# Latent attention of a two-block transformer: query squares summed on GpSimd, value blocks paired in one bank and copy, next query weights split behind the copies

## The chip, the cores and the metric

The kernel runs on one core of a Trainium2 chip. The metric is the device time of one execution in microseconds (us), the median of the runs. The five engines of a core work from queues of their own and wait for one another through semaphores: TensorE (PE; its weight loads are shown as PEld), VectorE (DVE), ScalarE (ACT), GpSimd (POOL) and SyncE (SP), which here issues the weight loads from memory. Matmul results go to PSUM, which has 8 banks of 512 float32 columns in each of 128 partitions; everything else is in SBUF.

## What is computed

The reference is a chain of two blocks on 512 tokens of width 1024: a first block (gated FFN, sliding-window attention beside a state-space layer, gated FFN), then a second one of two layers. The change lies in the mixer of the second block's first layer, a latent attention with 16 heads:

```
c_q = rms_norm(c_q, q_norm)                 # 512 wide
c_kv = rms_norm(c_kv, kv_norm)              # 256 wide
q = (c_q @ w_uq).reshape(B, S, 16, 128 + 64)
q_rope = apply_rope(q[..., 128:], cos, sin)
k_nope = (c_kv @ w_uk).reshape(B, S, 16, 128)
v = (c_kv @ w_uv).reshape(B, S, 16, 128)
for blk in range(4):                        # 128 queries against the keys up to them
    s = (q_nope @ k_nope + q_rope @ k_rope) * 192 ** -0.5
    pr = softmax(where(chunk mask, s, -1e30))
    outs.append(pr @ v)
```

All of it is float32.

## The kernel before

Every activation lies transposed, 128 features on the partitions and the 512 tokens along the row. A float32 product is made of three matmuls (`mm3`, lines 575 to 577): both operands are split into a high part (suffix H, or `uh` for weights) and a low part (L, or `ul`), and high x high, high x low and low x high are summed in PSUM. So each weight tile ("unit") that SyncE brings into one of three `raw` buffers is first cast by ScalarE into `uh` (line 548) and then VectorE writes what is left into `ul` (line 563). `feed_hi` and `feed_lo` are called at the place where a unit is used; their last number says how many units further ahead are to be cast or subtracted at that place. A unit of query weights (`uq`) is cast in two instructions, of 1024 and 512 columns.

The order of each engine's work is written out by hand in `latent_pe`, `latent_act` and `latent_dve`: a loop over `i`, in which even steps make the queries, keys and values for a pair of heads, and every step holds one head's scores, one head's transposes and one head's output, each from another head. One even and one odd step are a round.

- First comes `latent_first_...`: the two norms. ScalarE squares the four parts of the query latent into `qsq` (line 2318), and TensorE sums them over the partitions in `query_norm_pe`, with 16 matmuls of one column (line 2295). ScalarE's square root (line 2324) and VectorE's reciprocal (line 2355) make the factor `rq`, which the first softmax step (line 2459) needs.
- `queries_...`: queries of two heads (`QNH`, `QNL`), the rotary part (`QR`; ScalarE takes it out of PSUM with four copies, line 2263, VectorE rotates it, lines 2270 to 2274) and keys (`KNH`, `KNL`). `queries_turned_...` splits the rotated part into `QA` (lines 2394 and 2418), which the scores need.
- The values of a pair: `lin_tok` makes four blocks of 128 keys x 256 columns, each in a bank of its own, and ScalarE copies each to `VT` (line 2430).
- `latent_scores_pe` writes to banks 4 to 7; all the other results of the stage take turns on banks 0 to 3. A bank is taken again only when the result that held it has been read.
- `latent_softmax_...` and `latent_normalise_dve` work on the scores, `latent_turn_pe` transposes the ten 128x128 pieces into three banks (line 2491), `latent_turn_copy` copies them to `PTm` (ScalarE one bank, line 2509, VectorE two, line 2511), and `latent_output_pe` multiplies them with `VT` (line 2519). The output is split to `OH` and `OL` (lines 2529, 2533), which frees its bank.
- After step 10 the first half of the output projection follows (`mo` units), after step 17 the second.

GpSimd does nothing in the stage after it has multiplied the input by its norm (`latent_first_pool`, eight instructions of line 2364, done by 1214.4 us).

Of the kernel before, what the change touches and what calls it, by code (L numbers as in the profile page):

```python
# [11 lines left out]
MUL, ADD, SUB = ALU.mult, ALU.add, ALU.subtract  # L12
# [34 lines left out]
NOW = None  # L47
# [221 lines left out]
def program(nc, A, out):  # L269
    with ExitStack() as ctx:  # L270
# [262 lines left out]
        def feed_hi(e, name, ahead=1):  # L533

            u = done["act use"]
            assert units[u].name == name, (units[u].name, name)
            done["act use"] += 1
            ahead_hi(e, ahead)
# [1750 lines left out]

        def query_norm_pe(e):  # L2290
            b = bk.take(e, "qss")
            for n in range(4):
                for c in range(4):
                    s_fn.wait_ge(e, ("xq", "sq", c))
                    t = e.matmul(psum[:, b, n:n + 1], qsq[c][:, 128 * n:128 * n + 128], ones[:, 0:1], start=c == 0,
                                 stop=c == 3)
            t.then_inc(*s_mm.up("qss"))

        def latent_first_act(e):
# [59 lines left out]
        def latent_first_pool(e):  # L2359

            s_dv.wait_ge(e, ("x0", "r", 0))
            for k in range(8):
                s_lo.wait_ge(e, ("x0", k))
                e.tensor_tensor(HV[:, k, :], HV[:, k, :], R0, MUL).then_inc(*s_pool.up(("x0", k)))

        def queries_pe(e, p):
            u = lin(e, "uq", XQ, H2, ("qn", p, 0), cols=(0, 128), frees=False)
# [22 lines left out]
        def queries_turned_act(e, p):  # L2390
            s_dv.wait_ge(e, ("rope", "qr", p, 0))
            for hh in range(2):
                rows = slice(64 * hh, 64 * hh + 64)
                e.copy(QA[rows, hh, :], QR[rows, :]).then_inc(*s_hi.up(("qr", p, hh)))
            feed_hi(e, "uk", 1 if p == 1 else 2)

        def queries_dve(e, p):
            feed_lo(e, "uq", 2)
# [15 lines left out]
        def queries_turned_dve(e, p):  # L2414
            for hh in range(2):
                rows, other = slice(64 * hh, 64 * hh + 64), slice(64 - 64 * hh, 128 - 64 * hh)
                s_hi.wait_ge(e, ("qr", p, hh))
                e.tensor_tensor(QA[other, hh, :], QR[rows, :], QA[rows, hh, :].bitcast(F32), SUB).then_inc(
                    *s_lo.up(("qr", p)))
            feed_lo(e, "uk", 1 if p == 1 else 2)  # L2420

        def latent_values_act(e, p):
            feed_hi(e, "uv")
            if p:
                s_mm.wait_ge(e, ("mo", 2 * p - 1))
            else:
                cq_over(e)
            for i in range(4):
                s_mm.wait_ge(e, ("uv", p, i))
                e.copy(VT[:, i, :], P(("uv", p, i), 256)).then_inc(*bk.free(s_cp, ("uv", p, i), ("uv", p)))  # L2430

        def latent_scores_pe(e, h):
            p, hh = h // 2, h % 2
# [148 lines left out]
        def latent_pe(e):  # L2582
            latent_first_pe(e)
            bk.limit(4)
            for i in range(18):
                if i % 2 == 0 and i < 16:
                    queries_pe(e, i // 2)
                if i == 0:
                    query_norm_pe(e)
                if i >= 3:  # L2590
                    latent_output_pe(e, i - 3)
                if i == 0:
                    lin_tok(e, ("uv",), XK, [0, 128, 256, 384], 256, ("uv", 0))
                if i % 2 == 0 and 4 <= i <= 16:
                    lin_tok(e, ("uv",), XK, [0, 128, 256, 384], 256, ("uv", i // 2 - 1))
                if i == 10:
                    latent_project_pe(e, 0)
                if 2 <= i <= 17:
                    latent_turn_pe(e, i - 2)
                if i < 16:  # L2600
                    latent_scores_pe(e, i)
            bk.limit(8, 4)
            latent_project_pe(e, 1)
            first_layer_pe(e, "h1", "x10", "mo", (OH, OL, "o1"), [("mproj", 1, k) for k in LAST], 0)
# [25 lines left out]
        def latent_dve(e):  # L2630
            latent_first_dve(e)
            for i in range(19):
                if 2 <= i <= 17:
                    latent_normalise_dve(e, i - 2)
                if 1 <= i <= 16:
                    latent_softmax_dve(e, i - 1)
                if i % 2 == 0 and i < 16:
                    queries_dve(e, i // 2)
                if i == 18:
                    feed_lo(e, "mo", 2)  # L2640
                if i >= 3:
                    latent_output_dve(e, i - 3)
                if i % 2 == 0 and i < 16:
                    queries_turned_dve(e, i // 2)
                if i == 0:
                    feed_lo(e, "uv")
                    query_norm_dve(e)
                if i % 2 == 0 and 4 <= i <= 16:
                    feed_lo(e, "uv")
                if i == 10:  # L2650
                    latent_project_dve(e, 0)
                if 2 <= i <= 17:
                    latent_turn_copy(e, i - 2, False)
            latent_project_dve(e, 1)
            first_layer_dve(e, "x10", 0, latent_add(e))

# [1009 lines left out]
```

## Time and profile before

| | us |
|---|---|
| median of 3 runs | 2676.87 |
| lowest and highest run | 2675.57, 2677.82 |
| span of the profiled execution, first to last instruction | 2670.1 |
| median less this span | 6.8 |
| TensorE busy | 2620.4 (98%) |
| VectorE busy | 1676.6 (63%) |
| ScalarE busy | 1040.3 (39%) |
| GpSimd busy | 346.3 (13%) |

The profile gives of the profiled execution its span alone; its own time as a run is not listed. The latent stage lies between 1196 and about 1530 us of the span, its loop between 1232 and 1515. In timeline rows "[0.71 <-PE ps L577]" means that the engine had been idle for 0.71 us before this row and was released by the result of that line.

### The profile page before, as it was taken

The numbers are of one execution on the slowest core, as the hardware profiler recorded it, in microseconds if no ns is written. First come the engines' busy times: TensorE is split into PE (matmuls) and PEld (weight loads), VectorE is DVE, ScalarE is ACT, GpSimd is POOL, SyncE is SP. The second block draws the span as 40 slices with busy tenths as digits, with TensorE's granted clock in tenths as the row PEclk, the third lists the DMA queues.
The fourth block names the chain that finished last, engine by engine and source line by source line (L and its number), as shares of the span: only waits on it lengthen the run. The fifth ranks groups of instructions, "written<-read, shape, count | busy, mean of one in ns | idle before, by whom it ended". The sixth has DMA issues, their size and how long they took to land.

```text
span 2670.1 us, 35439 instructions
## 1 busy us (share of the span) xinstructions
PE 2620.4 (98%) x14660; PEld 2240.5 (84%) x14660; DVE 1676.6 (63%) x2567; ACT 1040.3 (39%) x1679; POOL 346.3 (13%) x361
## 2 busy tenths in 40 slices
PE   7999999999999999999999999999999999999999
PEld 7999999976688888888788798888879879888887
DVE  6754755768646534537866677647765377765765
ACT  4222233234434322235553454334353245433435
POOL 1133423020000000011000040000320014000031
PEclk9999999999999999999999999999999999999999
DMA  5243343521133232231121222322222212232322
GB/s 154 85 128 104 101 139 124 187 67 36 56 114 103 85 112 95 86 96 45 51 76 40 79 95 77 116 92 91 91 96 95 79 35 85 79 119 91 94 92 64
DMA packets 292728, 244.04 MB, mean 91 GB/s; under 512 B 19837, under 2 KB 285575, under 8 KB 292567
## 3 DMA queue, kind: packets, MB, share of 16 engines
q1 hardware_dynamic: 282503, 226.40, 26.9%
q0 software_dynamic: 5616, 13.22, 1.6%
q8 instruction: 116, 1.90, 0.3%
q10 hardware_dynamic: 4448, 2.16, 0.3%
q14 instruction: 45, 0.37, 0.0%
HBM read 230.70 MB, written 13.14 MB: 91 GB/s over the span
## 4 chain that ended last, share of the span: by engine, by line
PE 88%; DVE 6%; ACT 3%; issue 1%; DMA 1%; POOL 1%; SPq 0%; ACTq 0%; POOLq 0%; DVEq 0%
PE ps L575 27%; PE ps L576 26%; PE ps L577 26%; PE ps L777 1%; DVE ul L563 1%; PE ps L2519 1%; ACT uh L548 1%; PE ps L2491 1%; PE ps L3244 1%; PE ps L3220 1%; DVE rbuf L792 1%; PE ps L1592 0%; PE ps L1838 0%; PE ps L1936 0%; PE ps L1903 0%
## 5 line engine op out<-in xcount | busy, mean ns | idle before, releaser
L563 DVE TENSOR_TENSOR ul<-raw,uh 128x1024 fp32r<-128x1024 f32 (+3 forms) x416 | 527.3, 1291 | 337.0 <-ACT uh L548 336.4
L575 PE MATMUL ps<-OH,uh 128*128 128x512 f32 (+1 forms) x1736 | 646.5, 372 | 5.0 <-DVE ul L563 3.8
L577 PE MATMUL ps<-OH,ul 128*128 128x512 f32 (+1 forms) x1736 | 638.5, 368 | 0.0
L576 PE MATMUL ps<-OL,uh 128*128 128x512 f32 (+1 forms) x1736 | 638.4, 368 | 0.0
L548 ACT CAST uh<-raw 128x1024 fp32r<-128x1024 f32 (+3 forms) x416 | 412.0, 1025 | 163.6 <-PE ps L577 121.6
L575 PEld LDWEIGHTS ps<-OH,uh 128*128 128x128 f32 x1736 | 327.3, 189 | 68.2 <-issue 7.3
L576 PEld LDWEIGHTS ps<-OL,uh 128*128 128x128 f32 x1736 | 327.4, 189 | 55.1 <-issue 2.4
L577 PEld LDWEIGHTS ps<-OH,ul 128*128 128x128 f32 x1736 | 327.3, 189 | 54.7
L576 PE MATMUL ps<-HL,uh 128*128 128x512 f32 (+2 forms) x946 | 320.3, 339 | 0.0
L575 PE MATMUL ps<-HH,uh 128*128 128x512 f32 (+2 forms) x946 | 320.0, 338 | 0.0
L577 PE MATMUL ps<-HH,ul 128*128 128x512 f32 (+2 forms) x946 | 318.9, 337 | 0.0
L575 PE MATMUL ps<-XH,uh 128*128 128x264 f32 (+1 forms) x992 | 310.7, 313 | 3.4 <-DVE Q L862 1.5
L576 PE MATMUL ps<-XL,uh 128*128 128x264 f32 (+1 forms) x992 | 304.8, 307 | 0.0
L577 PE MATMUL ps<-XH,ul 128*128 128x264 f32 (+1 forms) x992 | 304.5, 307 | 0.0
L575 PEld LDWEIGHTS ps<-XH,uh 128*128 128x128 f32 x992 | 188.0, 189 | 22.8 <-issue 13.8
L575 PEld LDWEIGHTS ps<-HH,uh 128*128 128x128 f32 x946 | 177.7, 188 | 22.8 <-issue 0.9
L577 PEld LDWEIGHTS ps<-XH,ul 128*128 128x128 f32 x992 | 188.2, 190 | 8.5
L576 PEld LDWEIGHTS ps<-HL,uh 128*128 128x128 f32 x946 | 177.6, 188 | 20.9 <-issue 0.5
L577 PEld LDWEIGHTS ps<-HH,ul 128*128 128x128 f32 x946 | 177.9, 188 | 19.7
L576 PEld LDWEIGHTS ps<-XL,uh 128*128 128x128 f32 x992 | 188.1, 190 | 7.1
L808 POOL TENSOR_TENSOR acc<-acc,tmp 128x512 f32<-128x512 f32 (+2 forms) x56 | 69.3, 1238 | 672.2 <-ACT tmp L798 668.0
L2680 POOL TENSOR_TENSOR acc<-H 128x512 f32<-128x512 f32 x4 | 8.6, 2147 | 941.1 <-DVE H L2919 623.3
(450 smaller groups left out, 3757.7 us busy)
## 6 DMA issues: line engine op xcount, KB each, us to landing
raw<-in_ffn_w SPq DMA_DIRECT2D x40, 1024.0 KB, 5.0
raw<-in_ffn_w_up SPq DMA_DIRECT2D x40, 1024.0 KB, 4.9
raw<-in_ffn_w SPq DMA_DIRECT2D x32, 704.0 KB, 4.6
raw<-in_ffn_w_down SPq DMA_DIRECT2D x32, 704.0 KB, 4.5
raw<-in_w_in SPq DMA_DIRECT2D x16, 1024.0 KB, 5.4
raw<-in_gla_w_in SPq DMA_DIRECT2D x12, 1024.0 KB, 5.0
raw<-in_mla_w_o SPq DMA_DIRECT2D x8, 1024.0 KB, 5.0
raw<-in_ple_w_gate SPq DMA_DIRECT2D x8, 1024.0 KB, 5.3
```

The source lines that it names most:

```text
L548: e.copy(h, src).then_inc(*s_whi.up((u, j)))
L563: e.tensor_tensor(l, src, h.bitcast(F32), SUB).then_inc(*s_wlo.up(("unit", u)))
L575: e.matmul(o, wh, xh, start=first, stop=False)
L576: e.matmul(o, wh, xl, start=False, stop=False)
L577: return e.matmul(o, wl, xh, start=False, stop=last)
L777: i = e.matmul(psum[:, b, 0:n], ones[:, :], tile[:, t0:t0 + n], start=j == 0, stop=j == len(parts) - 1)
L792: e.reciprocal(r[:, t0:t0 + n], r[:, t0:t0 + n]).then_inc(*s_dv.up((tag, "r", hf)))
L808: e.tensor_tensor(a, a, tmps[k - 1][:, t0:t0 + n], ADD).then_inc(*s_pool.up(*((tag, "acc", k, hf) for hf in hfs)))
L2491: t = e.transpose(psum[:, b, o:o + 128], SS[h % 2][:, SO[n] + 128 * k:SO[n] + 128 * k + 128], ident[:, :])
L2519: t = e.matmul(psum[:, b, 128 * k:512], VT[:, k, 128 * (h % 2):128 * (h % 2) + 128], PTm[:, PO[k]:PO[k] + 512 - 128 * k], start=k == 0, st ...
L3220: e.matmul(psum[:, b, 0:256], KT[r:r + 64, s, 128 * h:128 * h + 128], GV[r:r + 64, s, 256 * h:256 * h + 256], start=True, stop=True).then_ ...
L3244: t = e.matmul(psum[:, bk.of[("hv", h, v)], 64 * n:64 * n + 64], cur[:, 128 * v:128 * v + 128], GQ[:, h, 64 * n:64 * n + 64], start=True, ...
```

## The change

Three edits, all in the latent stage.

1. GpSimd adds the four tiles of query squares into the first one, in three instructions, each waiting for the one before and for its square. TensorE waits for the last addition and sums over the partitions with 4 one-column matmuls in place of 16.
2. `latent_values_pe` takes the place of `lin_tok`: two blocks of 128 keys share a bank (columns 0 to 255 and 256 to 511), and ScalarE makes two copies of 512 columns in place of four of 256.
3. The query weights of the next pair are no longer cast and subtracted at the `uk` unit, ahead of the value copies, but behind the value copies on ScalarE and behind the `PTm` copies on VectorE (`ahead_hi` and `ahead_lo`). In the last step with values (`i` 16), VectorE's subtraction stays ahead of its copies.

```diff
         def query_norm_pe(e):
             b = bk.take(e, "qss")
+            s_pool.wait_ge(e, ("xq", "sum"))
             for n in range(4):
-                for c in range(4):
-                    s_fn.wait_ge(e, ("xq", "sq", c))
-                    t = e.matmul(psum[:, b, n:n + 1], qsq[c][:, 128 * n:128 * n + 128], ones[:, 0:1], start=c == 0,
-                                 stop=c == 3)
+                t = e.matmul(psum[:, b, n:n + 1], qsq[0][:, 128 * n:128 * n + 128], ones[:, 0:1], start=True, stop=True)
             t.then_inc(*s_mm.up("qss"))
...
+            s_fn.wait_ge(e, ("xq", "sq", 0))
+            for c in range(1, 4):
+                s_fn.wait_ge(e, ("xq", "sq", c))
+                s_pool.wait_ge(e, NOW)
+                e.tensor_tensor(qsq[0][:, 0:512], qsq[0][:, 0:512], qsq[c][:, 0:512], ADD).then_inc(
+                    *s_pool.up(("xq", "sum")))
...
-            feed_hi(e, "uk", 1 if p == 1 else 2)
+            feed_hi(e, "uk")
...
-            feed_lo(e, "uk", 1 if p == 1 else 2)
+            feed_lo(e, "uk")
+
+        def latent_values_pe(e, p):
+            xh, xl, tag = XK
+            u = next_unit(e, "uv")
+            hi, lo, _ = halves_of(u)
+            for k in range(2):
+                s_lo.wait_ge(e, (tag, k))
+            for i in range(2):
+                b = bk.take(e, ("uv", p, i))
+                for j in range(2):
+                    t0 = 256 * i + 128 * j
+                    for k in range(2):
+                        t = mm3(e, psum[:, b, 256 * j:256 * j + 256], xh[:, k, t0:t0 + 128], xl[:, k, t0:t0 + 128],
+                                hi[:, k, :], lo[:, k, :], k == 0, k == 1)
+                t.then_inc(*s_mm.up(("uv", p, i), *([("unit", u)] if i else [])))
 
         def latent_values_act(e, p):
-            feed_hi(e, "uv")
+            feed_hi(e, "uv", 0 if p else 1)
...
-            for i in range(4):
+            for i in range(2):
                 s_mm.wait_ge(e, ("uv", p, i))
-                e.copy(VT[:, i, :], P(("uv", p, i), 256)).then_inc(*bk.free(s_cp, ("uv", p, i), ("uv", p)))
+                e.copy(VT[:, 2 * i:2 * i + 2, :].rearrange("p a n -> p (a n)"), P(("uv", p, i))).then_inc(
+                    *bk.free(s_cp, ("uv", p, i), ("uv", p)))
+            ahead_hi(e, 1)
...
                 if i % 2 == 0 and 4 <= i <= 16:
-                    feed_lo(e, "uv")
+                    feed_lo(e, "uv", 0 if i < 16 else 1)
...
                 if 2 <= i <= 17:
                     latent_turn_copy(e, i - 2, False)
+                if i % 2 == 0 and 4 <= i < 16:
+                    ahead_lo(e, 1)
```

How the rows stand on the engines. ScalarE in an ordinary round (step `i` 4), from the output split to the `PTm` copies; `raw_49` holds the next query weights. Before:

```order
L2529 CAST OH<-ps 128x512
L2394 CAST QA<-tmp_58 64x512 x2
L548 CAST uh<-raw_49 128x4x256
L548 CAST uh<-raw_49 128x4x128
L2430 COPY VT<-ps 128x256 x4
L2509 COPY PTm<-ps 128x384
L2509 COPY PTm<-ps 128x128
```

After, the same stretch:

```order
L2550 CAST OH<-ps 128x512
L2398 CAST QA<-tmp_58 64x512 x2
L2449 COPY VT<-ps 128x512 x2
L548 CAST uh<-raw_49 128x4x256
L548 CAST uh<-raw_49 128x4x128
L2530 COPY PTm<-ps 128x384
L2530 COPY PTm<-ps 128x128
```

The two casts have moved from ahead of the value copies to behind them, and still stand ahead of the `PTm` copies.

VectorE in the same step, from the query split to the normalisation. Before:

```order
L2418 TENSOR_TENSOR QA<-tmp_58,QA 64x512 x2
L563 TENSOR_TENSOR ul<-raw_49,uh 128x4x256
L563 TENSOR_TENSOR ul<-raw_49,uh 128x4x128
L2511 COPY PTm<-ps 128x512
L2511 COPY PTm<-ps 128x256
L2475 RECIPROCAL zst<-zst 128x4
```

After:

```order
L2422 TENSOR_TENSOR QA<-tmp_58,QA 64x512 x2
L2532 COPY PTm<-ps 128x512
L2532 COPY PTm<-ps 128x256
L563 TENSOR_TENSOR ul<-raw_49,uh 128x4x256
L563 TENSOR_TENSOR ul<-raw_49,uh 128x4x128
L2496 RECIPROCAL zst<-zst 128x4
```

The two subtractions have changed places with the two copies.

ScalarE in the last step with values (`i` 16), where the unit is an output weight. Before:

```order
L2529 CAST OH<-ps 128x512
L548 CAST uh<-raw_51 128x1024
L2430 COPY VT<-ps 128x256 x4
L2509 COPY PTm<-ps 128x384
L2509 COPY PTm<-ps 128x128
```

After:

```order
L2550 CAST OH<-ps 128x512
L2449 COPY VT<-ps 128x512 x2
L548 CAST uh<-raw_51 128x1024
L2530 COPY PTm<-ps 128x384
L2530 COPY PTm<-ps 128x128
```

Here too the cast has moved behind the value copies; on VectorE the rows of this step stand as before.

## Rows read from the trace of the kernel before

**Rows 1.** The page: busy time of the engines; the chain that ended last.

```profile
PE 2620.4 (98%) x14660; PEld 2240.5 (84%) x14660; DVE 1676.6 (63%) x2567; ACT 1040.3 (39%) x1679; POOL 346.3 (13%) x361
...
PE 88%; DVE 6%; ACT 3%; issue 1%; DMA 1%; POOL 1%; SPq 0%; ACTq 0%; POOLq 0%; DVEq 0%
```

**Rows 2.** ScalarE's timeline, one round: start, duration, operation, idle time before.

```profile
1293.70 2.38 ACT L2263 COPY tmp<-ps 32x512 f32<-32x512 f32 x4 [2.01 <-PE ps L577]
...
1300.35 1.56 ACT L548 CAST uh<-raw 128x1024 fp32r<-128x1024 f32 x2
1301.82 1.19 ACT L2430 COPY VT<-ps 128x256 f32<-128x256 f32 x4
...
1321.44 2.38 ACT L2263 COPY tmp<-ps 32x512 f32<-32x512 f32 x4 [0.71 <-PE ps L577]
```

**Rows 3.** TensorE's timeline in that round, at the transposes.

```profile
1302.24 1.31 PE L2491 MATMUL ps<-ident,SS 128*128 128x128 f32 x10 [0.82 <-ACT VT L2430]
```

**Rows 4.** TensorE's timeline, the one-column sums and what follows.

```profile
1243.78 0.50 PE L2295 MATMUL ps<-ones,acc 128*128 128x1 f32 x4
...
1247.27 0.55 PE L575 MATMUL ps<-uh,CKH 128*128 128x256 f32 x1
```

**Rows 5.** Busy time in four stretches: PE, PEld, DVE, ACT, POOL; then clock, DMA.

```profile
1247.30:1250.60 3.30, 3.30 (x16) 3.30 (x17) 2.02 (x3) 3.11 (x6) 0.00 (x0) 0.50 0.01 2
1271.00:1274.60 3.60, 1.03 (x7) 0.79 (x8) 3.54 (x7) 1.88 (x4) 0.00 (x0) 1.00 0.02 9
1274.60:1277.90 3.30, 3.30 (x15) 3.20 (x14) 3.16 (x11) 0.53 (x3) 0.00 (x0) 0.50 0.00 0
1499.10:1503.00 3.90, 1.60 (x14) 1.40 (x13) 2.29 (x3) 3.37 (x8) 0.00 (x0) 1.00 0.00 0
```

**Rows 6.** Timelines of ScalarE and VectorE from the square root to the first softmax.

```profile
1247.44 0.26 ACT L2324 ACTIVATE misc<-ps,misc 128x4 f32<-128x4 f32 x1 [2.70 <-PE ps L2295]
...
1248.24 1.40 DVE L2418 TENSOR_TENSOR QA<-tmp,QA 64x512 fp32r<-64x512 f32 x2 [1.23 <-ACT QA L2394]
1249.95 1.83 DVE L563 TENSOR_TENSOR ul<-raw,uh 128x1024 fp32r<-128x1024 f32 x2 [0.30 <-ACT uh L548]
...
1252.63 0.35 DVE L2459 SCALAR_TENSOR_TENSOR SS<-ps,misc,MK 128x128 f32<-128x128 f32 x1 [0.56 <-PE ps L2444]
```

**Rows 7.** GpSimd's instructions of line 2364: duration in ns (min/median/max), first and last start.

```profile
L2364 POOL TENSOR_TENSOR H<-H,wk x8: 1290/1300/2278, 1201.9 to 1212.6; 128x512 f32<-128x512 f32 x8
```

**Rows 8.** Timelines around the squares: VectorE, ScalarE, and TensorE's first query matmul.

```profile
1211.82 1.42 DVE L2272 TENSOR_TENSOR tmp<-tmp,SIN 128x512 f32<-128x512 f32 x1
...
1229.08 0.61 ACT L2318 ACTIVATE tmp<-CQ 128x512 f32<-128x512 f32 x1
...
1230.67 1.83 DVE L563 TENSOR_TENSOR ul<-raw,uh 128x1024 fp32r<-128x1024 f32 x2 [1.65 <-ACT uh L548]
...
1232.55 0.50 PE L575 MATMUL ps<-CQH,uh 128*128 128x512 f32 x1 [0.33 <-DVE ul L563]
...
1244.40 0.69 DVE L2272 TENSOR_TENSOR tmp<-tmp,SIN 128x512 f32<-128x512 f32 x1
```

**Rows 9.** TensorE's timeline at the scores of step 2.

```profile
1274.01 0.39 PE L575 MATMUL ps<-KNH,QNH 128*128 128x256 f32 x1 [1.59 <-DVE QA L2418]
```

**Rows 10.** VectorE's timeline in the round of rows 2.

```profile
1301.53 1.83 DVE L563 TENSOR_TENSOR ul<-raw,uh 128x1024 fp32r<-128x1024 f32 x2
1303.27 1.01 DVE L2511 COPY PTm<-ps 128x512 f32<-128x512 f32 x2
```

**Rows 11.** TensorE's timeline at the start of the first projection half.

```profile
1386.00 0.50 PE L575 MATMUL ps<-OH,uh 128*128 128x512 f32 x1 [1.39 <-DVE ul L563]
```

**Rows 12.** Timelines of TensorE and VectorE in step 16.

```profile
1501.67 0.39 PE L575 MATMUL ps<-uh,CKH 128*128 128x256 f32 x1 [2.30 <-DVE OL L2533]
1504.03 2.40 PE L2519 MATMUL ps<-PTm,VT 128*128 128x512 f32 x8 [0.29 <-ACT PTm L2509]
...
1501.87 1.23 DVE L563 TENSOR_TENSOR ul<-raw,uh 128x1024 fp32r<-128x1024 f32 x1 [0.26 <-ACT uh L548]
```

More of the change, by code:

```diff
@@ L2592, in latent_pe @@
                 if i == 0:
-                    lin_tok(e, ("uv",), XK, [0, 128, 256, 384], 256, ("uv", 0))
+                    latent_values_pe(e, 0)
                 if i % 2 == 0 and 4 <= i <= 16:
-                    lin_tok(e, ("uv",), XK, [0, 128, 256, 384], 256, ("uv", i // 2 - 1))
+                    latent_values_pe(e, i // 2 - 1)
                 if i == 10:
```

## The prediction, as put on record before the result

> **What bounds the kernel now.** I read the page first: TensorE is busy 98% of the span and makes up 88% of the chain that ended last [rows 1]. So only two things shorten the run: fewer TensorE instructions, or less TensorE waiting. The change touches the latent-attention stage alone, 1232 to 1510 us, so I then read TensorE's waits there and, at each wait, the timelines of ScalarE and VectorE. The longest-run view says "TensorE waits"; the other two say how much of the wait would only move elsewhere.
>
> The stage is a ring of engines. In a round (two heads; one runs from 1293.70 to 1321.44, 27.7 us) TensorE makes queries and keys, ScalarE copies the rotary part out of PSUM, VectorE rotates, ScalarE and VectorE split it, TensorE scores, VectorE and ScalarE do the softmax. TensorE waits 0.82 us before its transposes for the four value copies [rows 3] (I count 1.0, since a next matmul starts some 0.2 before the one ahead has drained), and those copies stand on ScalarE behind a 1.56 us cast of the next query weights [rows 2]. But the rotary copies of the next round began only 0.71 us after ScalarE had been ready for them [rows 2]: without TensorE, the ScalarE and VectorE half of the ring needs 27.74 - 0.71 = 27.0 us. **So the 1.0 us can give at most 0.7 per round.** The round starting at 1293.70 began with 2.01 us of such slack [rows 2], because TensorE was late from the round before.
>
> **Part 1: query squares.** Before, 16 one-column matmuls (32 passes) take from 1243.78 to 1247.27, 3.49 us [rows 4]. After, 4 remain: 0.87 us, 2.6 us less on TensorE. The stretch behind them also ran at a granted clock of 0.50, the 1.2 GHz level, for 3.3 us [rows 5]; at full clock its 16 matmuls would have saved 16 x (0.21 - 0.12) = 1.4 us. On TensorE alone that makes 4.0 us.
>
> I do not count it, for what is late next is VectorE. It reached the first softmax step at 1252.63 with only 0.56 us of waiting for TensorE [rows 6]. Its chain ahead of that is rotation, key split, query split (ends 1249.64), weight subtraction (1.83), reciprocal. ScalarE's square root waited 2.70 us for the sums and held up the casts that the query split waits for: VectorE stood 1.23 us there, and 0.30 more for a cast [rows 6]. With the sums early these go: 1.23 + 0.30 + 0.56, less about 0.1 for the order of the casts: the first softmax could start 2.0 us earlier.
>
> Against it stands the price of three GpSimd additions. A GpSimd multiply of two 128x512 tiles took 1.30 us [rows 7], and while these ran a VectorE multiply of two SBUF tiles took 1.42 us, where the same instruction without GpSimd took 0.69 [rows 8]. The second addition can start when the second and third squares are there and the first addition is done: the third square ends at 1229.69 [rows 8], the first addition (from about 1229.0) at 1230.35, so the second runs 1230.4 to 1231.7. VectorE starts its subtraction for the first query weights at 1230.67 [rows 8], and TensorE's first query matmul waits for just that one, at 1232.55 [rows 8]. If VectorE waits the addition out, it and all behind it come 1.1 us later. Bounds: nothing (below nothing has no reason here, GpSimd shortens nobody), and the whole first two additions, 2.6. I take 1.1, since the 1.42 row is the same pair of operations. The third addition ends near 1237, long before 1244. **Part 1: -2.0 + 1.1 = -0.9 us.**
>
> The Trainium skill (SBUF — State Buffer, "Who interferes with whom") says that a VectorE instruction with two SBUF inputs contends with a GpSimd instruction that reads SBUF, and that the one which comes later fully blocks. The trace agrees: 1.42 against 0.69. Ordinary sharing of bandwidth would cost some half of it and leave Part 1 at -1.4.
>
> After this the second round's chain (softmax, three casts, query copy, rotation) is ScalarE and VectorE throughout, up to the scores at 1274.01, for which TensorE waited 1.59 us [rows 9]; the 0.9 is passed on whole, and TensorE just waits longer. The 3.3 us at clock 0.50 behind it [rows 5] may fall elsewhere: from 1.4 less (gone) to 1.0 more (all twenty score matmuls slow instead of fifteen). I take nothing.
>
> **Part 2: value copies before the cast, two per round.** Two 128x512 copies at about 0.55 us (four rotary copies of 512 columns took 2.38, 0.6 each) replace four in 1.19 [rows 2]. Now transposes need banks that the key split and the output split free, which are done by 1300.1; the third transpose bank and the next output wait for a copy each, with room. TensorE's 1.0 us goes in the four rounds that have it (1302, 1330, 1358, 1457).
>
> What is late next: VectorE. Before, it did subtraction and two copies without a gap, 1301.53 to 1304.2 [rows 10]. Now the copies come first (and must wait for the transposes, about 1301.9) and the subtraction waits for a cast that stands behind the second value copy, which waits for the last value matmul: copy 1301.46 to 1302.0, casts to 1303.0 and 1303.5, subtraction 1303.0 to 1304.85. That is 0.6 later than 1304.20. So in a round in which TensorE is not ahead, the half ring takes 27.0 + 0.6 = 27.65, a gain of 0.1. In the next round TensorE is 0.9 ahead, copies and casts come 0.9 earlier, the 0.6 vanishes, and the round takes 27.1: a gain of 0.65. Rounds from 1293, 1321, 1349: -0.1 - 0.65 - 0.65; the round from 1448, again with TensorE not ahead: -0.1. **Sum -1.5 us.** At the round from 1476 I find no difference.
>
> **Part 3: the two places where an output weight stands behind the values.** At 1386.00 TensorE waited 1.39 us for the subtraction of the first one [rows 11]. Before, its cast stood ahead of the value copies. Now it starts after them (the last value matmul goes at 1384.3, or 1383.4 with TensorE nearly 1 us ahead; copy to 1384.0), ends 1385.0, and a subtraction of 1.23 to 1.3 brings TensorE to 1386.35: **+0.35 us**, paid in full, for TensorE was waiting there. At 1501.67 TensorE waited 2.30 us for the output split to free a bank for the last value block [rows 12]. Now the values are done and the first transpose bank too, but the second needs that same split. Cast and subtraction of the output weight (1.23 from 1501.87) and then the copies (from 1503.2) stand before TensorE's output matmul at 1504.03 [rows 12]. VectorE's order is kept there (subtraction, then copies), while ScalarE's cast moves behind two value copies of 0.5: cast 1501.8 to 1502.85, subtraction to 1504.1, copies from 1504.2, output matmul at 1505.0. **+1.0 us**, because the wait that TensorE gave up is only turned into a later one.
>
> **Sum:** -0.9 - 1.5 + 0.35 + 1.0 = -1.05 us on a span of 2670.1. The runs shown take 2676.87, 6.8 us more than the profiled span; I keep that distance: **2675.8 us**.
>
> **Rivals.**
> 1. *TensorE gets all it is promised.* If VectorE and ScalarE have the room that I deny them: 4.0 (Part 1) + 4 x 1.0 + at 1501 six value matmuls and four transposes already done (1.2): -9.2, 2667.7 us. For it: 98% busy. Against: the 0.71 and the 0.56. 10%.
> 2. *GpSimd costs nobody anything, or the slow stretch after 1274 goes.* -1.1 or -1.4 more: about 2674.5. The squares might end at other times against VectorE. 18%.
> 3. *Slower: VectorE's new order and TensorE's clock.* Behind the 3.6 us in which TensorE was busy 1.03, it ran 3.3 us at 0.50 [rows 5]; in 3.9 us with 1.60 busy around 1501 it stayed at 1.00 [rows 5]. The change takes the last value matmuls out of that second stretch and adds 1.0 us of waiting: about 5 us with transposes only. If the clock falls there, some 2.2 us of output matmuls take up to twice as long, and as much again is possible behind the longer wait before 1386: +1.5 each. It decides when either stretch does fall: with one +0.5, with both +2 net, 2678.9 us. 17%.
>
> My forecast (between 2674.8 and 2677) gets 55%.
>
> **How the numbers follow.** The forecast's own bounds are -3.5 (no contention, no slow stretch) and +3. The range, **2671.5 to 2679.0**, leaves out rival 1 and a few per cent above, and the three runs before already spread over 2.3 us. About 0.2%, 5.4 us, is what a measurement of this kernel can tell from no change. Faster by more than that needs rival 1 or most of it: 0.10. Slower by more needs several of rival 3's prices at once: 0.03. Same: 0.87.
>
> **What would show each step.** Right: TensorE's wait for the value copies is gone, and a wait for the query split before the scores takes its place in the rounds after the first; the rotary copies follow each other every 27.1 us and ScalarE no longer waits before them; the VectorE subtraction at 1230 takes about 2.9 us instead of 1.83; the first softmax starts only about 0.9 us earlier though the sums are done over 1.5 us earlier; near 1504 TensorE waits for a VectorE copy. Wrong: rotary copies every 26.7 us (rival 1), an undisturbed subtraction (rival 2), or a granted clock of 0.50 behind 1386 or 1504 (rival 3). I would be wrong altogether if a bank wait which I take for covered, such as the output split before the second transpose bank, ended last in every round.

## The result: 0.14% slower, and the profile after

The changed kernel takes 2679.5 us (median of 20 runs, 2676.8 to 2685.5), the kernel before in the same comparison 2676.2 (20 runs, 2672.0 to 2683.5). The ratio is 1.0014, 95% interval 1.0008 to 1.0021. So it is slower by 0.08 to 0.21%: inside the 0.2% that I had called "same", but above the range, which ended at 2679.0. The likeliest case had the wrong sign.

The page of the changed kernel (span 2677.4 us), engine times and the chain that ended last, as in [rows 1]:

```profile
PE 2625.8 (98%) x14636; PEld 2242.3 (84%) x14636; DVE 1678.3 (63%) x2567; ACT 1040.0 (39%) x1663; POOL 349.9 (13%) x364
...
PE 86%; DVE 8%; ACT 3%; issue 1%; DMA 1%; POOL 1%; SPq 0%; ACTq 0%; POOLq 0%; DVEq 0%
```

TensorE has 24 instructions fewer and is busy 5.4 us longer; VectorE's share of the chain rose from 6 to 8%. More busy time for less work means slower matmuls, though some of it lies ahead of the stage (below). TensorE's waits in 1190 to 1620 us (total us, times, longest):

```profile
PE ps L575 <- DVE ul L563: 5.3, 3, 3.0
PE ps L2540 <- DVE PTm L2532: 2.3, 1, 2.3
PE ps L575 <- DVE OL L2554: 2.0, 5, 0.7
PE ps L575 <- DVE QA L2422: 1.9, 2, 1.6
PE ps L2512 <- DVE OL L2554: 1.8, 1, 1.8
```

The waits for the value copies [rows 3] are gone, and the largest wait is now for VectorE's subtraction of weights (`ul`), 3.0 us in one piece. The wait for the query split (`QA`) that I had foretold for the rounds is not there: the two waits of that kind lie ahead of the rounds, and 1.6 of the 1.9 us are those of step 2, as before.

To see where the time went I measured, in both traces, from the first rotary copies of the key (1208.67 us before, 1210.88 after; this start lay between 1207.9 and 1216.7 in the profiled executions of this study, ahead of anything the change touches). The span grew by 7.3 us: 2.2 ahead of that point, 4.5 in the stage, 0.6 behind it. The 2.2 are no effect of the change: the granted clock falls between 450 and 555 us in every profiled execution, here more often than in the kernel before. Inside the stage, from one point to the next:

| step | before | after | difference | predicted |
|---|---|---|---|---|
| to the first query matmul | 23.88 | 24.67 | +0.79 | +1.1 |
| on to ScalarE's rotary copies of the second round | 34.20 | 32.22 | -1.98 | -2.0 |
| on to those of the third round (scores of step 2 between) | 26.95 | 27.90 | +0.95 | 0 |
| four rounds of 27.7 us | 110.94 | 110.21 | -0.73 | -1.5 |
| rotary copies to first projection matmul | 9.10 | 10.31 | +1.21 | +0.35 |
| on to the rotary copies behind it | 62.78 | 64.43 | +1.65 | 0 |
| last rotary copies to the output of head 14 | 27.51 | 28.43 | +0.92 | +1.0 |
| on to the output of head 15 | 11.52 | 13.20 | +1.68 | 0 |
| sum | | | +4.5 | -1.05 |

Three rows for which I forecast nothing make 4.3 us. In all three TensorE ran at the 1.2 GHz level for a while (in the first of them in the kernel before too, but for less time). Busy time of the engines in five stretches (columns as in [rows 5]):

```profile
1277.00:1281.00 4.00, 4.00 (x14) 3.60 (x14) 2.94 (x8) 1.70 (x6) 0.00 (x0) 0.56 0.00 0
1384.00:1388.40 4.40, 1.43 (x12) 1.22 (x11) 3.10 (x5) 3.83 (x6) 0.00 (x0) 1.00 0.10 34
1388.40:1392.00 3.60, 3.57 (x11) 2.87 (x12) 1.11 (x1) 2.50 (x3) 0.00 (x0) 0.69 0.33 104
1506.00:1509.00 3.00, 0.78 (x6) 0.55 (x6) 1.92 (x3) 1.60 (x4) 0.00 (x0) 1.00 0.00 0
1509.00:1512.00 3.00, 2.95 (x4) 1.35 (x5) 1.60 (x6) 0.00 (x0) 0.00 (x0) 0.54 0.00 0
```

The second and the fourth are the waits (TensorE busy 1.43 of 4.40 us and 0.78 of 3.00), the third and the fifth what follows: granted clock 0.69 and 0.54. TensorE's own timeline at the two places, to be held against [rows 11] and [rows 12]:

```profile
1388.43 0.50 PE L575 MATMUL ps<-OH,uh 128*128 128x512 f32 x1 [3.00 <-DVE ul L563]
1388.77 0.40 PE L576 MATMUL ps<-OL,uh 128*128 128x512 f32 x1
...
1390.47 0.63 PE L576 MATMUL ps<-OL,uh 128*128 128x512 f32 x1
```

```profile
1505.91 0.88 PE L2512 MATMUL ps<-ident,SS 128*128 128x128 f32 x6 [1.78 <-DVE OL L2554]
1509.05 4.09 PE L2540 MATMUL ps<-PTm,VT 128*128 128x512 f32 x8 [2.27 <-DVE PTm L2532]
```

The eight output matmuls that took 2.40 us [rows 12] take 4.09.

### The profile page after: what moved, and what is told of

The parts are those of the page before. It is cut to its first block, busy times and chain, and to the rows that moved or that the text cites. A ratio compares the mean times of both kernels' runs of the same rounds, so it can differ in the third digit from the quotient of the medians.

```text
span 2677.4 us, 35378 instructions
## 1 busy us (share of the span) xinstructions
PE 2625.8 (98%) x14636; PEld 2242.3 (84%) x14636; DVE 1678.3 (63%) x2567; ACT 1040.0 (39%) x1663; POOL 349.9 (13%) x364
## 4 chain that ended last, share of the span: by engine, by line
PE 86%; DVE 8%; ACT 3%; issue 1%; DMA 1%; POOL 1%; SPq 0%; ACTq 0%; POOLq 0%; DVEq 0%
PE ps L575 27%; PE ps L576 26%; PE ps L577 26%; DVE ul L563 1%; PE ps L777 1%; PE ps L2540 1%; ACT uh L548 1%; DVE zst L2483 1%; DVE SS L2480 1%; PE ps L3267 1%; PE ps L3243 1%; DVE rbuf L792 1%; PE ps L1592 0%; PE ps L1838 0%; PE ps L1936 0%
```

## The experiments

**My theory:** the orders of VectorE and ScalarE at two places (step 10, step 16) make TensorE wait longer, and its clock falls behind the longer waits. **The first rival:** the clock falls by chance, and what costs is the waiting itself. **The second rival:** edit 1, with GpSimd's additions, is to blame. Each kernel was timed in alternation with the kernel before; the ratios have intervals of about plus or minus 0.0009. There are three series, on three chips: the orders of steps 10 and 16 and the filled waits; then the two halves, the late additions and the first run of all mends; then the last three. The changed kernel itself ran in none of them, so against it I compare ratios to the kernel before; such a comparison carries both intervals, together about 0.11%, some 3 us.

### The halves of the change

Edit 1 alone: the kernel before with GpSimd's additions and 4 one-column matmuls, the rest left as it was.

> The kernel before with edit 1 alone (three GpSimd additions, 4 one-column matmuls for 16). Theory (VectorE is late next, and the additions hold it up once): the first rotary copies come 0.8 us later, those of the second round 1.2 us earlier; of that, 0 to 1.2 us is left at the end, depending on where the clock's slow stretch behind the scores of step 2 falls: 0 to 1.2 us faster than before. Rival (TensorE alone counts): 4 us faster.

Measured: 2673.56 us (before 2675.83), ratio 0.9995 (0.9985 to 1.0004).

Edits 2 and 3 alone: the changed kernel with the squares summed by TensorE again.

```diff
-            s_pool.wait_ge(e, ("xq", "sum"))
...
+                for c in range(4):
+                    s_fn.wait_ge(e, ("xq", "sq", c))
+                    t = e.matmul(psum[:, b, n:n + 1], qsq[c][:, 128 * n:128 * n + 128], ones[:, 0:1], start=c == 0,
+                                 stop=c == 3)
```

> The changed kernel without edit 1: 16 one-column matmuls, no GpSimd additions. Theory: both long waits of steps 10 and 16 and their slow stretches are there, so 3 to 5 us slower than before. Rival (GpSimd's additions cause the loss): equal to before.

Measured: 2679.51 us (before 2675.83), ratio 1.0017 (1.0009 to 1.0025). The whole loss is here, and the second rival falls: edit 1 alone costs nothing measurable and its trace has the gain that I had worked out (second round's rotary copies 1.2 us earlier). The 4 us of its own rival lie at the very edge of the interval, but the trace does not show them.

### Undoing the order at one place

Step 10, the cast and the subtraction of the first output weight ahead of the value copies again:

```diff
-            feed_hi(e, "uk")
+            feed_hi(e, "uk", 2 if p == 5 else 1)
...
-            feed_lo(e, "uk")
+            feed_lo(e, "uk", 2 if p == 5 else 1)
```

> The changed kernel, with the cast and the subtraction of the first output weight (step 10) put back ahead of the value copies. Theory 1: TensorE's wait before the first projection falls from 3.0 us to about 1.9 (the 1.4 of before and 0.5 that TensorE is ahead), and the clock stays at 1.00 there: 1.2 + 1.6 = 2.8 us faster than the changed kernel, 0.5 slower than before. Theory 2 (waits alone): 1.2 faster than the changed kernel.

Measured: 2677.51 us (before 2676.33), ratio 1.0003 (0.9995 to 1.0012). From the rotary copies to the first projection matmul it takes 9.10 us again, as before; TensorE's wait and what follows it:

```profile
1385.12 0.50 PE L575 MATMUL ps<-OH,uh 128*128 128x512 f32 x1 [1.81 <-DVE ul L563]
1385.46 0.40 PE L576 MATMUL ps<-OL,uh 128*128 128x512 f32 x1
```

By the ratios this is 0.11%, 2.9 us, below the changed kernel, give or take 3: it cannot tell theory 1 (2.8) from theory 2 (1.2). In this execution the clock stayed at 1.00 behind the shorter wait of 1.8 us, but that is not what the order does each time. The version with both mends, below, has the same order and the same wait (1.77 us, first projection matmul at 1382.47), and there it fell. Busy times around the first projection matmul, here and then there:

```profile
1381.10:1385.10 4.00, 2.21 (x19) 2.00 (x17) 3.87 (x6) 3.95 (x7) 0.00 (x0) 1.00 0.34 120
1385.10:1389.10 4.00, 3.98 (x17) 3.30 (x18) 1.23 (x1) 2.95 (x4) 0.00 (x0) 1.00 0.31 99
```

```profile
1378.50:1382.40 3.90, 2.19 (x19) 1.99 (x17) 3.80 (x6) 3.85 (x6) 0.00 (x0) 1.00 0.32 114
1383.30:1386.70 3.40, 3.40 (x10) 2.66 (x9) 0.55 (x1) 2.13 (x3) 0.00 (x0) 0.55 0.46 141
```

Step 16, the other way: ScalarE's cast of the output weight behind its copies of transposes, VectorE's subtraction behind the normalisation of step 17. So TensorE's output matmul waits for neither.

```diff
-            ahead_hi(e, 1)
+            if p < 7:
+                ahead_hi(e, 1)
...
+                if i == 16:
+                    ahead_hi(e, 1)
...
+                if i == 17:
+                    ahead_lo(e, 1)
...
-                    feed_lo(e, "uv", 0 if i < 16 else 1)
+                    feed_lo(e, "uv", 0)
```

> The changed kernel, with the output weight of step 16 cast behind ScalarE's PTm copies and subtracted on VectorE behind the next normalisation, so that nothing stands ahead of the PTm copies. The output matmul behind it can then start some 2.3 us earlier. Theory 1: those 2.3 us and the slow stretch behind (1.6) go: 3.5 to 4 us faster than the changed kernel. Theory 2 (waits alone): 2.3 faster. Rival: the weight now comes late for the second projection half, and half of it comes back as a wait there.

Measured: 2673.88 us (before 2676.33), ratio 0.9989 (0.9980 to 0.9999). TensorE's timeline:

```profile
1505.03 0.87 PE L2513 MATMUL ps<-ident,SS 128*128 128x128 f32 x6 [1.76 <-DVE OL L2555]
1505.74 2.37 PE L2541 MATMUL ps<-PTm,VT 128*128 128x512 f32 x8
```

The wait of 2.27 us is gone and the eight matmuls take 2.37 us, not 4.09. From the last rotary copies to the output of head 15 it takes 37.5 us (before 39.0, after 41.6). This one order is worth 0.25%, 6.7 us, against the changed kernel, give or take 3: more than the change lost, and more than the 3.5 to 4 of theory 1, which the trace bears out (4.1). The rival falls: behind the output of head 15 the run takes 1155.3 us, in the changed kernel 1155.2.

Both together:

> The changed kernel with both repairs, of step 10 and of step 16. Theory 1 (additive): 6 to 6.5 us faster than the changed kernel, so 2.5 to 3 us faster than the kernel before (ratio 0.999). Theory 2: 3.5 faster than the changed kernel, equal to before.

Measured: 2673.07 us (before 2676.33), ratio 0.9986 (0.9977 to 0.9995), 0.28% or 7.5 us below the changed kernel. That fits theory 1 and is more than theory 2 allows, but over the mend of step 16 alone (0.9989) a gain from step 10 is not shown.

### The waits kept, the engine kept busy

To part the clock from the waiting, I left all orders as in the changed kernel and let TensorE do useless matmuls into a free bank during the two waits, 12 ahead of the projection and 8 ahead of the output of step 17:

```diff
+            for _ in range(n):
+                e.matmul(psum[:, bank, 0:512], KRH[:, 0:128], KRH[:, 0:512], start=True, stop=True)
...
+                if i == 17:
+                    busy_pe(e, 4, 8)
...
                 if i == 10:
+                    busy_pe(e, 4, 12)
```

Measured: 2676.97 us (before 2676.33), ratio 0.9996 (0.9986 to 1.0006), 0.18% or 4.8 us below the changed kernel's. TensorE's timeline and the busy times at both places:

```profile
1508.91 2.39 PE L2540 MATMUL ps<-PTm,VT 128*128 128x512 f32 x8 [0.42 <-DVE PTm L2532]
```

```profile
1389.80:1393.40 3.60, 3.51 (x15) 2.90 (x16) 1.17 (x2) 2.58 (x3) 0.00 (x0) 1.00 0.29 95
1505.70:1508.80 3.10, 2.73 (x14) 2.03 (x14) 1.87 (x4) 1.75 (x4) 0.00 (x0) 1.00 0.00 0
1508.80:1511.80 3.00, 2.89 (x15) 2.13 (x16) 1.65 (x6) 0.46 (x1) 0.00 (x0) 1.00 0.00 0
```

The output of head 14 comes no earlier (28.45 us behind the rotary copies, against 28.43), for it waits for the same copy; but it runs at clock 1.00. Twenty matmuls more, and the time is less: the clock behind the waits costs, not the waits alone. The first rival falls for these two places. The size, 4.8 us, is more than the 3.3 us which the one profiled execution shows there; the interval (some 3 us either way) covers both.

### GpSimd's additions later, and all mends together

The additions wait until VectorE has written the last low part of the query latent, so they no longer lie over the first query weights:

```diff
             s_fn.wait_ge(e, ("xq", "sq", 0))
+            s_lo.wait_ge(e, ("xq", 3))
```

> The changed kernel, with GpSimd's additions held until VectorE has written the last low part of the query latent (about 1235 us), past the weight subtraction that TensorE's first query matmul waits for. Theory (the second addition held VectorE up by 0.8 us): that subtraction takes 1.83 us again instead of 2.63, TensorE's wait there falls from 1.56 to 0.76 and everything up to the second round's scores comes 0.8 us earlier. Of the whole, 0 to 0.8 faster than the changed kernel. Rival (the third addition then does the harm instead, on the key rotary part and the next weights): no gain or slower.

Measured: 2676.57 us (before 2675.83), ratio 1.0007 (0.9999 to 1.0016). The first query matmul stands at 23.87 us again, and the subtraction ahead of it takes what it took before (VectorE's timeline):

```profile
1229.91 1.83 DVE L563 TENSOR_TENSOR ul<-raw,uh 128x1024 fp32r<-128x1024 f32 x2 [1.65 <-ACT uh L548]
```

The 0.8 us is real in the trace (the second round's rotary copies too come 0.8 us earlier, 56.1 us behind those of the key for 56.9); that it shortens the run is not shown (the intervals overlap). The additions still hold VectorE up, only later, where TensorE does not wait for it. VectorE and GpSimd in this version:

```profile
1234.16 1.77 DVE L2349 TENSOR_TENSOR KRL<-tmp,KRH 128x512 fp32r<-128x512 f32 x1 [0.21 <-ACT KRH L2318]
```

```profile
1234.09 1.29 POOL L2368 TENSOR_TENSOR acc<-acc,acc 128x512 f32<-128x512 f32 x1 [20.45 <-DVE CQL L846]
1235.52 3.26 POOL L2368 TENSOR_TENSOR acc<-acc,tmp 128x512 f32<-128x512 f32 x2
```

That subtraction takes 0.69 us in the kernel before.

Steps 10 and 16 mended and the additions later, run twice:

> The changed kernel with both repairs and the late additions. Theory: 6.5 to 7 us faster than the changed kernel, 3 to 3.5 faster than the kernel before. Rival (rounds bound by VectorE absorb it): no better than the two repairs alone.

Measured: 2671.04 us (before 2675.83), ratio 0.9983 (0.9975 to 0.9992). It is faster than the kernel before, but against the two repairs alone (0.9986) the rival stands: no gain of the late additions is shown.

> The version with both repairs and late additions once more, beside the filled one: 4.5 us faster than the kernel before, as in the first series.

Measured: 2671.92 us (before 2675.94), ratio 0.9988 (0.9980 to 0.9997). Here the second round's rotary copies stand at 56.1 us, 2.0 ahead of before: just the gain which the prediction had worked out without GpSimd's interference. By the ratio it is 3.2 us faster than the kernel before, where 4.5 was expected; the interval covers both.

The same with 19 useless matmuls at the places where TensorE still waits: 5 ahead of the last transposes of head 0, 7 ahead of the scores of step 2, 7 ahead of the first projection.

```diff
+                if h == 0 and ks[0] == 2:
+                    busy_pe(e, 4, 5)
...
+                    busy_pe(e, 4, 7)
...
+                if i == 2:
+                    busy_pe(e, 4, 7)
```

> The changed kernel with both repairs, the late additions, and matmuls without a use in the waits that are left: 5 ahead of the third transpose bank and 7 ahead of the scores of step 2 (TensorE waited 1.4 and 1.6 us there), and 7 ahead of the first projection half (1.8). Theory 1 (the clock falls behind these waits in some executions and not in others): no slow stretch is left in the stage, and the median falls below that of the version without the filling by 1 to 3 us, 6 us faster than the kernel before. Theory 2 (the ring of ScalarE and VectorE is what sets the time there): equal to the version without the filling.

Measured: 2668.45 us (before 2675.94), ratio 0.9972 (0.9962 to 0.9981). **This is the fastest version, ahead of both kernels**; its nine runs lie within 2666.3 to 2671.3. The gain over the version without the filling, 3.5 us in the same series, is a little above what theory 1 gave (1 to 3), and its condition is met: in the profiled execution the granted clock is 1.00 through the whole stage. Busy times from the last transposes of head 0 to the end of the scores of step 2, and around the projection:

```profile
1265.80:1271.70 5.90, 5.63 (x28) 3.91 (x26) 4.91 (x9) 3.98 (x8) 0.00 (x0) 1.00 0.41 136
1271.70:1275.30 3.60, 3.60 (x22) 3.30 (x22) 3.46 (x11) 0.49 (x2) 0.00 (x0) 1.00 0.00 0
1377.60:1381.40 3.80, 3.73 (x25) 3.08 (x23) 3.71 (x5) 3.75 (x6) 0.00 (x0) 1.00 0.29 103
1381.40:1385.00 3.60, 3.52 (x15) 2.93 (x16) 1.25 (x2) 3.05 (x4) 0.00 (x0) 1.00 0.26 63
```

Last, the filling of step 2 alone, in the kernel before:

> The kernel before with the same 12 matmuls without a use in step 2 alone. Theory 1: the slow stretch behind the scores of step 2 goes, 1.4 us faster in the executions that had it in this place, 0.5 to 2.5 us in the median. Theory 2: no difference, since ScalarE's slack of 2.0 us in the next round shows that the slow stretch was off the path.

Measured: 2675.67 us (before 2675.94), ratio 1.0000 (0.9991 to 1.0009): no difference. The stretch behind the scores ran at full clock, but in this execution an earlier stretch had fallen (rotary copies of the second round at 59.6 us instead of 58.1) and ate it. I cannot tell from it what the filling is worth there: the interval, 2.4 us either way, covers most of what theory 1 gave (0.5 to 2.5).

### The places over all profiled executions

From point to point, in us; bold where the granted clock fell in the stretch. The last column is the whole stage, from the first rotary copies of the key to the output of head 15:

| kernel | key's to second round's rotary copies | second to third rotary copies | projection to rotary copies | output of head 14 to 15 | whole stage |
|---|---|---|---|---|---|
| before | **58.08** | **26.95** | 62.78 | 11.52 | 306.9 |
| edit 1 alone | 56.90 | 25.38 | 62.82 | **11.99** | 305.3 |
| before, step 2 filled | **59.60** | 25.39 | 62.83 | **12.28** | 308.1 |
| after | 56.89 | **27.90** | **64.43** | **13.20** | 311.4 |
| edits 2 and 3 alone | **59.55** | 25.41 | **64.39** | **14.44** | 312.8 |
| additions later | 56.11 | **28.16** | 62.79 | **14.25** | 310.3 |
| step 10 mended | 56.93 | **27.85** | 62.78 | **13.01** | 308.3 |
| step 16 mended | 56.90 | 25.38 | **64.31** | 11.50 | 304.6 |
| both mended | 56.90 | 25.38 | **64.41** | 11.52 | 303.5 |
| all, first run | 56.08 | **26.77** | **64.38** | 11.52 | 304.0 |
| all, second run | 56.14 | **27.80** | 62.83 | 11.51 | 303.6 |
| after, waits filled | 56.93 | **26.95** | 62.83 | 11.51 | 307.2 |
| all, filled | 56.15 | 25.39 | 62.80 | 11.52 | 301.3 |

Four things are to be read here. A fall is not a property of the kernel alone: at one place one kernel has it in one execution and not in another (all, first and second run). Ahead of the projection that holds for the waits of 1.8 us (2 of 4 executions) and of 3.0 us (3 of 4) alike; with the old order's 1.39 us it came in none of three, and with the wait filled in neither of two. So that the change made the fall likelier there is plausible; that putting the order of step 10 back takes it away is not shown. At the output of head 15 it came in all four executions with the 2.3 us wait and in none of the six without the wait or with it filled. And the old order is not free of it either: of the three kernels that have it (the first three rows) two fell there. The column shows +0.5 and +0.8 us for them, but their fall begins ahead of the output of head 14, which comes 28.17 and 27.94 us behind the last rotary copies instead of 27.51: in all they pay 1.1 and 1.2 us, where the changed order pays +1.5 to +2.9. So the pair of profiles at the top, in which before had no fall there, overstates the difference at this place, and the medians are the better witness.

The fourth thing stands in the first column. Behind the one-column sums the clock fell in all three kernels with 16 of them and in none of the ten with 4. And it did not fall behind a wait there: TensorE was busy without a gap with the one-column matmuls when it came. Busy times in the kernel before with step 2 filled, where the sums run from 1249.36 to 1253.38:

```profile
1249.00:1252.00 3.00, 3.00 (x28) 2.92 (x26) 2.68 (x5) 1.29 (x3) 0.00 (x0) 1.00 0.00 0
1253.00:1256.00 3.00, 3.00 (x15) 3.00 (x16) 1.37 (x2) 2.40 (x5) 0.00 (x0) 0.50 0.00 0
```

In this execution and in that of edits 2 and 3 alone the second round's rotary copies come 1.5 us later than in the kernel before, whose fall there was shorter. So edit 1 is worth 1.2 us against the one profile of before, and 2.7 against these two.

The Trainium skill (TensorE: Matmul & The Clock Gate, "What's actually happening") says that the number of slow matmuls at the start of a kernel varies from run to run of the same kernel; in the middle of this one the traces show the same (64.38 and 62.83). It adds that the penalty of that start is under 1% of a typical span and not worth fitting; here the two falls of the changed kernel at steps 10 and 16 cost 3.3 us, 0.12%, and yet that is more than the sum of all that the change otherwise does (+0.2 us, below).

## Why the prediction failed, point by point

**GpSimd's additions: right, 0.79 us for 1.1.** The additions ran where I had worked them out: less the 2.21 us by which this trace is late, the second one takes 1230.3 to 1231.6, and VectorE's subtraction starts at 1230.65, 0.34 us behind the start of the second and with 0.96 us of it to come. The first of its two instructions took 2.03 us where it had taken 1.23, so VectorE lost 0.80 us, less than the whole 0.96. GpSimd and VectorE in the changed kernel:

```profile
1230.89 1.48 POOL L2367 TENSOR_TENSOR acc<-acc,acc 128x512 f32<-128x512 f32 x1 [14.31 <-ACT acc L2316]
1232.52 1.30 POOL L2367 TENSOR_TENSOR acc<-acc,tmp 128x512 f32<-128x512 f32 x1
```

```profile
1232.86 2.63 DVE L563 TENSOR_TENSOR ul<-raw,uh 128x1024 fp32r<-128x1024 f32 x2 [1.64 <-ACT uh L548]
...
1237.92 1.50 DVE L2349 TENSOR_TENSOR KRL<-tmp,KRH 128x512 fp32r<-128x512 f32 x1 [0.21 <-ACT KRH L2318]
```

2.63 us where it was 1.83 [rows 8]. The second case is cleaner: a subtraction of two 128x512 tiles in SBUF took 1.50 beside the third addition (1237.45, 1.41 us), and the same instruction 0.69 in the kernel before: again 0.81 us lost with 0.94 us of the addition to come.

**The earlier softmax: right, 1.98 us for 2.0**, so Part 1 gave -1.2 in place of -0.9. The first softmax step itself comes 42.8 us behind the key's rotary copies, where it had come 44.0. The one-column sums take some 0.8 us, and the stretch behind them ran at 1.00 where it had been at 0.50 [rows 5]:

```profile
1247.60:1250.90 3.30, 3.09 (x25) 2.89 (x24) 3.20 (x6) 2.41 (x5) 0.00 (x0) 1.00 0.03 7
```

As predicted that gave nothing beyond what VectorE let through.

**The scores of step 2: I took nothing, this execution shows +0.95.** The stated bound was 1.0 more. Over the executions it is anything from 0 to 2.8 us above the undisturbed 25.38. Without filling the clock fell there in seven of eleven, once of twice with the old order of the rounds and in six of nine with the new one, so the +0.95 is not shown to come from the change.

**The rounds: right mechanism, wrong size, 0.73 us for 1.5.** The first and the fourth round gave nothing (27.76 and 27.76, before 27.74), the second and the third 0.39 and 0.38 instead of 0.65. In the first round VectorE reaches its reciprocal 11.20 us behind the rotary copies, before 10.50: 0.7 later, where I had 0.6. ScalarE's timeline shows the rotary copies:

```profile
1295.67 2.39 ACT L2263 COPY tmp<-ps 32x512 f32<-32x512 f32 x4 [2.04 <-PE ps L577]
...
1323.43 2.38 ACT L2263 COPY tmp<-ps 32x512 f32<-32x512 f32 x4
...
1350.78 2.39 ACT L2263 COPY tmp<-ps 32x512 f32<-32x512 f32 x4
```

Where the kernel before had 0.71 us of waiting for TensorE [rows 2], there is none: ScalarE and VectorE bound the round, as predicted. The failed term is TensorE's lead. I had it 0.9 to 1 us ahead after one round; the gains say 0.4, so some 0.2 us of VectorE's later subtraction is left in each of these rounds. One cause may be that TensorE now waits for that subtraction at the keys too, 0.25 and 0.21 us in the two rounds (weight loads of TensorE, the first of them):

```profile
1322.69 0.19 PEld L575 LDWEIGHTS ps<-CKH,uh 128*128 128x128 f32 x1 [0.25 <-DVE ul L563]
```

**The first projection: +1.21 for +0.35.** The same lead enters here: I let the last value matmul go 0.9 us earlier. TensorE's row for it, in the kernel before and in the changed one:

```profile
1384.33 0.28 PE L577 MATMUL ps<-uh,CKL 128*128 128x256 f32 x1
```

```profile
1385.15 0.28 PE L577 MATMUL ps<-uh,CKL 128*128 128x256 f32 x1
```

Measured from the rotary copies of the round (1376.90 and 1378.12) that is 7.43 and 7.03: a lead of 0.40, so 0.5 of the 0.9 is missing. The chain behind it, ScalarE's and VectorE's:

```profile
1385.46 0.59 ACT L2449 COPY VT<-ps 128x512 f32<-128x512 f32 x1 [0.52 <-PE ps L577]
```

```profile
1387.15 2.36 DVE L563 TENSOR_TENSOR ul<-raw,uh 128x1024 fp32r<-128x1024 f32 x2 [1.24 <-ACT uh L548]
```

From the start of that matmul to the projection's first (1388.43) it takes 3.28 us, where I had 2.95 (1383.4 to 1386.35), mainly because the copy can start only 0.31 after the matmul does. 0.35 + 0.50 + 0.33 = 1.18, which is the measured 1.21 within the reading. Undoing the order gave back just these 1.21 us (9.10 again).

**Step 16: right, +0.92 for +1.0.** TensorE's output matmuls waited 2.27 us for VectorE's copies, as foretold.

**The clock behind the two waits: the step that failed.** The sum has nothing for it, and 3.3 of the 5.5 us between forecast and profile are this; 1.6 are TensorE's lead and the chain at the projection (0.8 in the rounds, 0.9 at the projection), 1.0 is step 2, and the rest gives 0.4 back. It was rival 3, "+1.5 each", 2678.9 us, at 17%. Measured: +1.65 and +1.68 in the profile. Mechanism, places and price were right; the chance was wrong. That 2678.9 is so near the measured 2679.5 is in part luck: the rival put both falls at +2 net against a kernel before of 2676.87, and the kernels differ by 3.3 us in the medians and by 4.5 in the stage. I argued that TensorE had stayed at 1.00 through the before kernel's long wait around 1501 [rows 5], one execution in which it did not fall; the two other kernels with that order fell at the same place. In the changed order it fell in seven of eight cases (three of four behind 3.0 us, four of four behind 2.3). And I weighed the waits by one example each way, when the row [rows 5] at 1271 to 1277 had already shown a fall behind a wait of 1.59 us. Without the clock the sum of the measured terms is -1.2 - 0.73 + 1.21 + 0.92 = +0.2 us: the change gives and takes back, and the clock decides its sign. That balance is of these two profiles. What stays open is how often the clock falls at each place; one profile for each kernel is too few to give a rate.

**The range.** The forecast's own upper bound was +3, which on 2676.87 is 2679.9 us, but the range was closed at 2679.0. The measured 2679.5 lies between the two.

## What to carry to other kernels

When an edit on one engine turns a short wait of TensorE into one of 2 to 3 us, price the matmuls behind that wait at half clock as part of the likeliest case, not as a remote rival, even where the present trace shows one such wait that went unpunished. When copies are put ahead of a cast, look in every round for the one whose weight is wanted next: four equal rounds gained 0.7 us together, and two unequal places lost 2.1 us. Gains of a ring of engines are not summed over its rounds but followed to the next place where an engine waits: of the lead of 0.9 us that I carried to the projection only 0.4 was there.

## What was not expected of the hardware

Twenty useless matmuls of 128x512 put into two waits made the run 4.8 us shorter than the changed kernel's by their ratios (give or take 3), and nineteen, at three places, brought the best version from 0.9988 to 0.9972 in the same series, some 3.5 us by the medians, though no useful instruction changed its place in the order. And the spread of a kernel's runs seems to be mostly this clock: the kernel before ran between 2671.5 and 2683.1 us in the last series with a mean granted clock of 0.996 in its fastest run and 0.992 in its slowest (over its 25 runs time and clock have a correlation of -0.89), while the filled version stayed within some 5 us at 0.995 to 0.998.
